# HGRN level products that stream 128 columns, and a last layer without its context queries

## The reference

```python
def hgrn_scan(q, k, v, log_f, s0, want_out):
    ...
    def step(s, inp):
        k_n, v_n, lf_n = inp[0], inp[1], inp[2]
        bcum = jnp.cumsum(lf_n, axis=2)
        b_last = bcum[:, :, -1]
        s_next = s * jnp.exp(b_last)[..., None] + jnp.einsum(
            "bhcd,bhce->bhde", k_n * jnp.exp(b_last[:, :, None] - bcum), v_n)
        if want_out:
            q_n = inp[3]
            dec = jnp.exp(jnp.where(incl[:, :, None], bcum[:, :, :, None, :] - bcum[:, :, None, :, :], -jnp.inf))
            att = jnp.einsum("bhid,bhjd,bhijd->bhij", q_n, k_n, dec)
            o = jnp.einsum("bhcd,bhde->bhce", q_n * jnp.exp(bcum), s) + jnp.einsum("bhij,bhje->bhie", att, v_n)
            return s_next, o
        return s_next, None
...
    for l in range(DEPTH):
        want_ctx = l < DEPTH - 1
        ...
        y_x, y_c = mixing_layer(hx, hc, ..., want_ctx)
        x = x + g1x * rms_norm(y_x, norm_mix_post[l])
        ...
    return x
```

## Time and profile before

| | us |
|---|---|
| median of 3 runs | 3452.58 |
| lowest and highest | 3436.17, 3452.72 |
| the profiled execution | 3425.4 |
| its span, first to last instruction | 3423.6 |

### The profile page before, as it was taken

How to read it: one execution, slowest core, us unless ns; L and a number is a source line. 1 busy time by engine, 2 the same in 40 slices (tenths; PEclk the granted TensorE clock), 3 DMA queues, 4 the chain that set the end, 5 groups by cost and what they waited for, 6 DMA issues and landing times. The chain is left out here.

```text
span 3423.6 us, 36943 instructions
## 1 busy us (share of the span) xinstructions
PE 3073.0 (90%) x16216; PEld 2423.6 (71%) x16216; DVE 1296.3 (38%) x1898; ACT 916.0 (27%) x1248; POOL 216.9 (6%) x222
## 2 busy tenths in 40 slices
PE   6967879899998998999997986879899998989997
PEld 3646869656784767888885556869556994758886
DVE  1434426100672525243343434436011652453444
ACT  3172111130114534222223253111221013442222
POOL 1001220200001100000000001120200001100000
PEclk8989899899999999999998987979899659999999
DMA  5111040211321011221111010000011001013221
GB/s 196 38 37 62 1 148 1 87 49 50 111 101 40 1 50 37 69 67 62 62 62 37 26 49 1 1 1 1 25 49 37 1 2 40 25 62 96 93 95 62
DMA packets 143351, 174.21 MB, mean 51 GB/s; under 512 B 5382, under 2 KB 116744, under 8 KB 143063
## 3 DMA queue, kind: packets, MB, share of 16 engines
q1 hardware_dynamic: 142240, 171.39, 15.1%
q0 software_dynamic: 672, 0.37, 0.1%
q10 hardware_dynamic: 279, 0.09, 0.0%
HBM read 169.74 MB, written 2.10 MB: 50 GB/s over the span
## 5 line engine op out<-in xcount | busy, mean ns | idle before, releaser
L482 PE MATMUL ps<-modulated,weights 128*128 128x512 f32 (+3 forms) x2080 | 697.5, 498 | 18.6 <-ACT modulated L994 11.3
L482 PEld LDWEIGHTS ps<-modulated,weights 128*128 128x128 f32 (+1 forms) x2080 | 399.8, 193 | 312.5 <-issue 282.3
L891 PE MATMUL ps<-region_r 128*128 128x512 f32 (+1 forms) x1536 | 376.4, 353 | 0.0
L891 PEld LDWEIGHTS ps<-region_r 128*128 128x128 f32 x1536 | 270.7, 188 | 41.0
L891 PE MATMUL ps<-modulated_r,region_r 128*128 128x512 f32 (+1 forms) x768 | 233.6, 359 | 19.7 <-DVE modulated_r L1596 19.4
L891 PE MATMUL ps<-mixed_r,region_r 128*128 128x512 f32 (+1 forms) x768 | 231.6, 356 | 0.0
L891 PE MATMUL ps<-mixed_r,weights_r 128*128 128x512 f32 (+1 forms) x768 | 231.1, 356 | 0.0
L891 PE MATMUL ps<-region_r,weights_r 128*128 128x512 f32 (+1 forms) x768 | 229.5, 353 | 0.0
L737 PEld LDWEIGHTS ps<-region 128*128 128x128 f32 x1344 | 206.9, 249 | 15.9 <-DVE region L1483 7.5
L737 PE MATMUL ps<-region 128*128 128x64 f32 x1344 | 209.8, 334 | 3.3 <-DVE region L1483 3.3
L1270 DVE TENSOR_TENSOR weights_r<-weights,region_r 128x2048 fp32r<-128x2048 f32 x64 | 146.5, 2288 | 146.8 <-ACT region_r L972 146.8
(11 more groups left out here) (278 smaller groups left out, 4114.0 us busy)
## 6 DMA issues: line engine op xcount, KB each, us to landing
weights<-in_w_mlp SPq DMA_DIRECT2D x64, 1024.0 KB, 5.3
weights<-in_w_ada SPq DMA_DIRECT2D x40, 1024.0 KB, 5.3
weights<-in_w_in SPq DMA_DIRECT2D x34, 1024.0 KB, 5.0
region<-in_w_ada SPq DMA_DIRECT2D x8, 1024.0 KB, 16.4
weights<-in_w_out SPq DMA_DIRECT2D x8, 1024.0 KB, 5.3
modulated<-in_x SPq DMA_DIRECT2D x1, 2048.0 KB, 16.6
out<-region SPq DMA_DIRECT2D x4, 512.0 KB, 2.7
region<-in_k_mask SPq DMA_DIRECT2D x1, 1344.0 KB, 6.9
```

Source lines behind the costliest of these rows:

```text
L482: last = mm(dst[0:m, CTX + a:CTX + b], w[:, k, m0:m0 + m], rhs[:, k, a:b], start=(first and k == 0), stop=(final and k == ks - 1))
L891: last = mm(dst[:, CTX + a:CTX + b], w[:, k, m], r[:, a:b], start=(k == 0 and r is r_low), stop=(k == KB - 1 and w is low))
```

## The change

Two things are changed.

First, in both layers, a level product streams both halves of the query blocks, 128 columns instead of 64. The columns of the half that isn't wanted land beside the wanted 64, in the slot of the neighbouring product, and the next product of the row overwrites them; so for d = 0 the row is walked backwards, and the last product of each row still streams 64. DVE reads the same 64 columns as before.

Second, in the last layer, all that serves only context queries goes: the 256-column products of qkv units 0 to 3, hq, cq and uq, and those of the norms of q and cq; the convolution and silu of the context part of q; in GDN, for chunks 0 and 1 and both directions, L617 (key/query) with its mask, exponential and product, and L656 with its exponential and POOL's product with q; in HGRN the diagonal and the level products of the context pair, with the widening of its queries and its copies. The keys of that pair are still widened, now in an instruction with a wait on its own end (`link`).

```diff
@@
+        def pairs_out(l):
+            return [p for p in range(NPAIR) if 2 * p in chunks_out(l)]
+        def level_items(l):
+            return len(chunks_out(l)) + NLEV * len(pairs_out(l))
...
@@ POOL
-                        mask_and(T_[:, 2 + ci % 2], madd[1 - d], g_[:, ci, d, :])
-                        mask_and(TT[:, 2 + ci % 2], madd[d], ng[:, ci, d, :]).then_inc(gmask_ready, 1)
+                        last = mask_and(T_[:, 2 + ci % 2], madd[1 - d], g_[:, ci, d, :])
+                        if ci in chunks_out(l):
+                            last = mask_and(TT[:, 2 + ci % 2], madd[d], ng[:, ci, d, :])
+                        last.then_inc(gmask_ready, 1)
...
-                        pool.wait_ge(eg_exp, base + ci + 1)
+                        if ci not in chunks_out(l):
+                            continue
+                        pool.wait_ge(eg_exp, o_count(l, d, -1) + outs_upto(l, ci))
                         nc.gpsimd.tensor_tensor(T_[:, ci], T_[:, ci], qT[:, :, 128 * ci:128 * ci + 128], ALU.mult).then_inc(qd_ready, 1)
@@ PE
-                    gemm(l, "qkv", i, [2 * i, 2 * i + 1], Hm, h_before=16 * l if i == 0 else None)
+                    gemm(l, "qkv", i, [2 * i, 2 * i + 1], Hm, lo if i < 2 else 0, h_before=16 * l if i == 0 else None)
...
-                        for h in range(H):
+                        for h in range(H if ci in chunks_out(l) else 0):
                             last = mm(ps[:, QK, 128 * h:128 * h + 128], kT[:, h, cc], qT[:, h, cc], start=True, stop=True)
...
-                        for h in range(H):
+                        for h in range(H if ci in chunks_out(l) else 0):
                             mm(ps[:, G, 128 * h:128 * h + 128], la[:, ci, d, h:h + 1].to_broadcast([128, 128]), tri[d], start=True, stop=True)
...
-                    gemm(l, "hq", i, [2 * i, 2 * i + 1], Hm)
+                    gemm(l, "hq", i, [2 * i, 2 * i + 1], Hm, lo)
...
-                    for i in range(NLEV * NPAIR):
-                        lv, p = divmod(i, NPAIR)
+                    for i, (lv, p) in enumerate((lv, p) for lv in range(NLEV) for p in pairs):
+                        bank = (diagonals + i) % 6
...
                         pe.wait_ge(m_ready, mb + i + 1)
-                        pe.wait_ge(lv_evac, eb + i + 1)
+                        if diagonals + i >= 6:
+                            pe.wait_ge(lv_evac, eb + diagonals + i - 5)
...
-                        for r in range(2 * H):
+                        for r in (range(2 * H) if d else range(2 * H)[::-1]):
                             ci, h = 2 * p + r // H, r % H
-                            last = mm(ps[:, i % 6, 64 * r:64 * r + 64].rearrange("p (n s) -> p n s", n=blocks_of),
-                                      HK[d][:, h, 128 * ci:128 * ci + 128], q5[:, h, blocks_of * ci:blocks_of * (ci + 1), 1 - d, :],
+                            spare = r > 0 if d == 0 else r < 2 * H - 1
+                            first = 64 * r - (64 if spare and d == 0 else 0)
+                            of = slice(None) if spare else slice(1 - d, 2 - d)
+                            ne = 2 if spare else 1
+                            last = mm(ps[:, bank, first:first + 64 * ne].rearrange("p (e n s) -> p e n s", e=ne, n=blocks_of),
+                                      HK[d][:, h, 128 * ci:128 * ci + 128],
+                                      q5[:, h, blocks_of * ci:blocks_of * (ci + 1), of, :].rearrange("p n e s -> p e n s"),
                                       start=True, stop=True)
...
-                gemm(l, "cq", 0, [0, 1], Hm)
+                gemm(l, "cq", 0, [0, 1], Hm, lo)
...
-                    last = project(free_pair(l, "uq", h), w, CQ, 2, 96 * h, 96)
+                    last = project(free_pair(l, "uq", h), w, CQ, 2, 96 * h, 96, lo)
@@ DVE
-                        for p in range(NPAIR):
-                            i = NPAIR * lv + p
-                            dve.wait_ge(lv_out, lvb + NC + i + 1)
+                        for p in [p for p in range(NPAIR) if p not in pairs]:
+                            widen(d, lv, p, False)
+                        for j, p in enumerate(pairs):
+                            i = len(pairs) * lv + j
+                            dve.wait_ge(lv_out, lvb + diagonals + i + 1)
                             dve.wait_ge(m_ready, mb + i + 1)
-                            widen(d, lv, p)
+                            widen(d, lv, p, True)
```

More of the change, by code:

```diff
@@ L243, in trunk_program, with outs_upto, m_base, lv_base @@
         NLEV, NPAIR = len(LEVELS), NC // 2
-        NLV, NEV, NM = 2 * NC + NLEV * NPAIR, NC + NLEV * NPAIR, NPAIR * (NLEV + 1)
+        def pairs_out(l):
+            return [p for p in range(NPAIR) if 2 * p in chunks_out(l)]
+        def level_items(l):
+            return len(chunks_out(l)) + NLEV * len(pairs_out(l))
+        def outs_upto(l, ci):
+            return len([c for c in chunks_out(l) if c <= ci])
+        def m_base(l, d):
+            return sum(2 * len(pairs_out(k)) * (NLEV + 1) for k in range(l)) + d * len(pairs_out(l)) * (NLEV + 1)
+        def lv_base(l, d):
+            return sum(2 * (level_items(k) + NC) for k in range(l)) + d * (level_items(l) + NC)
+        def evac_base(l, d):
+            return sum(2 * level_items(k) for k in range(l)) + d * level_items(l)
         def o_count(l, d, n):
@@ L717, in _ @@
                 for d in range(2):
-                    mb, eb = NM * (2 * l + d), NEV * (2 * l + d)
+                    mb, eb = m_base(l, d), evac_base(l, d)
+                    diagonals, pairs = len(chunks_out(l)), pairs_out(l)
                     if d == 1:
@@ L721, in _ @@
                     pe.wait_ge(k_done, 2 * l + d + 1)
-                    for ci in range(NC):
+                    for bank, ci in enumerate(chunks_out(l)):
                         cc = slice(128 * ci, 128 * ci + 128)
                         for h in range(H):
-                            last = mm(ps[:, ci, 128 * h:128 * h + 128], HK[d][:, h, cc], HQ[:, h, cc], start=True, stop=True)
+                            last = mm(ps[:, bank, 128 * h:128 * h + 128], HK[d][:, h, cc], HQ[:, h, cc], start=True, stop=True)
                         last.then_inc(lv_out, 1)
-                    for i in range(NLEV * NPAIR):
-                        lv, p = divmod(i, NPAIR)
+                    for i, (lv, p) in enumerate((lv, p) for lv in range(NLEV) for p in pairs):
+                        bank = (diagonals + i) % 6
                         if l == 0 and p == 0:
@@ L1095, in _ @@
                         act.wait_ge(p1_exp_in, base + ci + 1)
[L1096 to L1097 removed]
+                        last = af(T_[:, ci % 2], T_[:, ci % 2], ACT.Exp, bias=zero_col)
+                        if ci in chunks_out(l):
+                            last = af(TT[:, ci % 2], TT[:, ci % 2], ACT.Exp, bias=zero_col)
+                        last.then_inc(p1_exp, 1)
                     act.wait_ge(p1_done, base + NC)
@@ new lines, in widen @@
+                    last = v.tensor_tensor(k5[:, :, :, k, :], k5[:, :, :, k, :], by[:, :, :, q].unsqueeze(3).to_broadcast([128, H, n, s]), ALU.mult)
+                    if queries:
+                        last.then_inc(m_ready, 1)
+                    else:
+                        link(last)
+                for d in range(2):
+                    lvb, mb, eb = lv_base(l, d), m_base(l, d), evac_base(l, d)
+                    diagonals, pairs = len(chunks_out(l)), pairs_out(l)
+                    for bank, ci in enumerate(chunks_out(l)):
+                        dve.wait_ge(lv_out, lvb + bank + 1)
+                        v.tensor_tensor(HATT[:, ci], ps[:, bank, :].rearrange("p (h d) -> p h d", h=H), over_heads(ident), ALU.mult).then_inc(lv_evac, 1)
```

104 lines of the change are left out of this document (55 added, 49 removed).

## The result

The changed kernel takes 3313.43 us (median of 4 runs, 3307.13 to 3326.34), the kernel before 3452.65 (4 runs beside it, 3436.17 to 3494.45): a ratio of 0.9617, 95% interval 0.9568 to 0.9666. That is faster by 3.8%. The forecast was 3322 in a range of 3285 to 3360.

The account below looks back on a forecast made before the run. PE was taken as the bound, at half clock in the last layer's HGRN levels; terms summed to 130.6 us, giving 3294.8 against the profiled 3425.4 and 3322 against the median; own range 3295 to 3345, 8-in-10 range 3285 to 3360.

Parts of the forecast that it names:

- What bounds the kernel: Whole kernel: PE busy 90% of the span, no other engine over 38%; last layer's HGRN stage at clock 0.51.
- Strided columns at no cost: HGRN level products: a pass of 128 strided columns takes 0.117 us, as the strided 64 hide fully.
- Rivals B and C: Level products: strided streaming in proportion, 3409, chance 0.06 with the stretch up to C; or more than that, about 3530, 0.03.
- The 1 us charged for the first layer: First layer's level products: 128 columns instead of 64 cost 1 us more, taken off the summed gain.
- The levels: Last layer's HGRN stage becomes DVE's: 44.7 us from diagonals to scan, a gain of 32.4 and 32.8, together 65.2 us.
- Rival A: Last layer's levels: the clock stays at half, passes take 0.212 us, 31 us less gain, 3353; chance 0.10.
- The second scan: Last layer's HGRN, second direction: scan at full clock since the levels no longer end at half, a gain of 5.2 us.
- GDN: Last layer without context queries: 7.6 us in the first parts and 12.4 where W is made, either within 3 us.
- Projections: Last layer without context queries: 13.8 us in qkv, 13.8 in hq, 6.9 in cq, 3.4 in uq.
- The total: Whole kernel: gains of 130.6 us after 1 us off for the first layer; forecast chance 0.81.

## Why the prediction was right

**What bounds the kernel.** Right. The levels in the last layer were bound by PE at half clock, and the projections got shorter by what PE does for the context queries; in GDN it was the waits of PE for POOL and DVE that got shorter, as the forecast had it.

**Strided columns at no cost.** Right: 0.116 us a pass, the same 59.8 us a direction in the first layer before and after. Rivals B and C are out by the same row. The page cited for it, "SBUF — State Buffer" of the Trainium skill, section "Door 1: The DMA port swizzle", said so; the trace agrees nearly, with 0.118 us a pass in the first level, where every second fp32 is read, against 0.116 with 64 columns. The 1 us charged for the first layer was 0.

**The levels.** Right in mechanism and size: 45.0 us a direction for 44.7, DVE's part from 2617.91 on 37.1 us for 36.9. Taken apart, the wide products alone give 21 of the 32 us of a direction, the cuts alone 21 as well, and each of them misses the last 11: without the width PE at half is the bound, without the cut DVE with three pairs.

**Rival A** did not happen; the kernel with the cuts alone is A made to happen, with its 11 us a direction. Its rule was that of the Trainium skill, "TensorE: Matmul & The Clock Gate", section "What's actually happening", the clock set by how busy PE has been. The runs disagree if busy means time: busy 34.23 of 44.90 us at 1.00 with 128 columns, 34.60 of 36.10 at 0.53 with 64. PE's pauses are not beside the point either: the products of GDN's first part have 128 columns, PE is busy 20.29 of 35.20 us there, and the clock was 0.82. And one reading of the forecast was not exact: right before the stretch at half the level products did not run "without a pause"; 0.33 us stand ahead of it in the earlier trace rows.

**The second scan.** The 5.2 us came, but their step failed: "I expect full clock for both, since the levels no longer end at half". Behind levels at full clock the scan ran at 0.51 (wide products alone), behind levels at half it ran at 1.00 (cuts alone). So this term came out by luck. From the second scan's start to the sums behind it, all ten traces with two pairs a level show 10.6 us, the four with three pairs 15.9 to 17.9: what gave the 5.2 us goes with the cut of the context pair and not with the levels' clock. Why, no run settles.

**GDN.** Of 20.0 us, 18.3 came. The first parts and W hold (21.4 against the kernel before, 21.7 undone by themselves); the earlier trace rows put the third `kbg` 8.55 us after the first, and POOL's timeline now has it 2.39 us after:

```profile
2195.11 2.04 POOL L444 TENSOR_TENSOR mixed<-region,gdn_small 128x512 f32<-128x512 f32 x2 [76.57 <-ACT region L1145]
2197.50 1.04 POOL L444 TENSOR_TENSOR mixed<-region,gdn_small 128x512 f32<-128x512 f32 x1 [0.36 <-PE ps L687]
```

The sum lacked a term: the two scans behind W got 3.1 us longer together. The text had named such a thing, a clock that moves in GDN with the earlier start, as what no term holds. The granted clock makes the length; the second scan before, then after:

```profile
2411.80:2447.40 35.60, 28.49 (x192) 26.66 (x192) 7.97 (x23) 4.87 (x7) 10.13 (x10) 0.83 0.00 1
2394.60:2433.40 38.80, 31.72 (x193) 29.54 (x193) 8.00 (x23) 4.87 (x7) 10.03 (x10) 0.72 0.00 1
```

In the first trace of the kernel before the scans took 39.0 and 35.6 us, in its other two traces 35.5 to 35.7 each. With the context queries of GDN cut they took 38.8 twice in eight traces, but 36.0 and 34.4 in the ninth, that of the kernel with narrow products in the first layer. So the 3.1 us are no fixed price of the cut: against the other two traces of the kernel before, GDN's gain is 15.0 and 16.4 us, and the last layer's 129.5 and 129.7.

**Projections.** Right: 13.6, 13.8 and, with the scan and the sums, 18.0 for 17.3. The unit of hq now comes every 6.87 us, word for word the figure read from the earlier trace rows:

```profile
2486.94 0.60 ACT L1168 ACTIVATE region<-ps 128x512 f32<-128x512 f32 x1 [5.91 <-PE ps L509]
2493.81 0.60 ACT L1168 ACTIVATE region<-ps 128x512 f32<-128x512 f32 x1 [6.27 <-PE ps L509]
```

**The total.** 131.6 for the last layer against 132.7 measured. The misses (GDN's scans -3.1, its first parts and W +1.4, MLA and the end +2.7) are small and of both signs, and cancel in part; how near the sum came is luck to that extent. What the forecast had no idea of is in the spread: over all its executions here (58) the kernel before takes 3417 to 3514 us, 24 of them over 3480, the changed kernel (8) 3293 to 3326. By the medians, 3456.5 and 3309.7, the change is worth 147 us and not the 132.7 of the stages it was meant for. That narrow products in the first layer cost 29 to 67 us in some executions is shown; that they make up all of the 14 us more is not.

## What to carry to other kernels

Where many short passes run back to back, read the granted clock beside the pass time before counting passes: if it is half, try the columns that a pass has to spare, even for results nobody reads. Then see which engine stands second: here either edit alone stops 11 us short, and only both together free PE and DVE. And before a difference between two traces is explained, see it in a second execution of the same kernel: 20 us in the first layer were nothing of the change.

## What was not expected of the hardware

- A pass of 128 columns, contiguous or every second block, costs 0.116 to 0.118 us, one of 64 columns 0.114 to 0.116 at full clock and 0.215 at half. In the level products the columns beyond 64 are free, and with them the clock held; in GDN's first part, with pauses of 3 us, passes of 128 columns ran at 0.82.
- With narrow passes the clock fell even with PE idle between them (4.24 of 6.60 us busy ahead of the fall in the third level), and under wide passes it came back though PE never paused.
- The first layer's levels at 64 columns fall in some executions and not in others: five of ten directions in the five traces that have only narrow products there, of three kernels. With all or every second product wide they fell in no trace. With five narrow levels of seven two of four runs lay over 50 us above the other two; there is no trace of such a run.
- The first layer's MLP takes 542.1 to 543.7 us or 552.2 to 553.8 us for the same 3072 passes at a granted clock of 0.99, in kernels with and without the change. What sets it stays open.
